# Weight loads that wait for exactly the chunk that last used their buffer; turned blocks of the up projection's first half taken one chunk on

## The chip, the cores and the metric

One core of one Trainium2 chip runs the kernel. The metric is the device time of one execution in microseconds; lower is better. The kernel before took 2496.27 us (median of three executions, 2493.42 to 2497.68).

## The reference

Two transformer blocks run one after the other on x of 256 tokens by 2048 features, all in float32. What matters here is the first block's feed-forward part, on `rms_norm(h)` of 256 x 2048:

```python
def conv_gated_mlp(u, w_up, conv_w, conv_b, w_down):
    '''up-projection -> causal depthwise conv (width 3) -> GELU gate * value -> down-projection.'''
    S = u.shape[1]
    up = u @ w_up
    pad = jnp.pad(up, ((0, 0), (CONV_WIDTH - 1, 0), (0, 0)))
    up = conv_b + sum(pad[:, j:j + S] * conv_w[j] for j in range(CONV_WIDTH))
    gate, val = jnp.split(up, 2, axis=-1)
    return (jax.nn.gelu(gate, approximate=True) * val) @ w_down
```

`w_up` is 2048 x 11264 and `w_down` is 5632 x 2048. Around it stand the mixers, output projections, an embedding gate and, in the second block, a gated feed-forward of the same size without a convolution (phase "glu" below).

## The kernel before

**Chunks.** Every weight matrix is streamed in chunks of 1 MB (128 partitions x 2048 floats; 512 input rows by 512 columns), 428 in all, grouped in phases (`PHASES`). Phase "up" has 11 iterations of 8 chunks; chunks 0 to 3 of an iteration give 512 gate columns (the first half), chunks 4 to 7 the 512 value columns (the second half). The queue SP issues the load of a chunk into one of four buffers `raw0` to `raw3` (`load`, buffer j % 4). ACT rounds it to `w_hi` (`high`, L645), DVE subtracts to get the remainder `w_lo` (`low`, L1662), and PE multiplies with both (L1208 to L1210). `w_hi` and `w_lo` have two buffers each, so ACT's copy for chunk j+2 waits until PE has finished chunk j. The stretch on ACT from that copy to the next is called slot j here; extra work given for j in a stream's `at` table runs on ACT or DVE behind slot j's copy or subtraction.

**When a load may start.** A load waits until DVE has finished the chunk `back` before it: `c - back + 1` chunks done. With four buffers the last user of a buffer is normally four chunks back. A phase whose number of chunks before it is not a multiple of four shifts this: phase "pe1" has two chunks, so the first two chunks of "up" reuse buffers whose last user is two chunks back. `stream_plan` takes for each j the smallest distance over all iterations of a phase, which for "up" gives back = [2, 2, 4, 4, 4, 4, 4, 4], in every one of its 11 iterations. Phases "pg1" and "pg2" (two iterations each) have the same list; "down1" to "down2" have 4 except where a phase begins two chunks off.

**The turned blocks.** The up projection comes out with tokens on partitions; the convolution wants columns on partitions. For each half, ACT copies the result from PSUM to `up_rows` (`up_evacuation`, L910, slots 3 and 7). DVE transposes 32 x 32 blocks (`turn_up`, L2155). SP stores the blocks to DRAM (`put_up_blocks`, L434) and reads them back rearranged with four transfers (`take_up_blocks`, L440); ACT then copies them to `ff_sum` (`up_columns`, L918). The convolution (`affine` on ACT, L929; `convolve` on DVE, L2166), the GELU (`gelu_gate`, L936), the product on POOL (`up_products`, L605), its rounding on ACT (`product_high`, L955) and its remainder on POOL (L608) follow in the next iteration.

**SP's order.** SP executes in order, and its steps for the blocks of iteration i stand among the loads of iteration i+1: load 0, put first half, load 1, take first half, loads 2 to 4, put second half, load 5, take second half, loads 6 and 7. Each load stands some four chunks ahead of its multiplication. A wait in any of these holds all that follow.

**Loops.** On SP iterations 0 and 1 of "up" are written out and the rest is a loop; on ACT iteration 0 is written out. The blocks of iteration 10 are handled among the loads of "down1", whose back is 4 everywhere.

Of the kernel before, what the change touches and what calls it, by code (L numbers as in the profile page):

```python
# [49 lines left out]
RAW = 4  # L50
# [23 lines left out]
def stream_plan():  # L74


    plan, chunk, group, used = {}, 0, 0, [0] * RAW
    last = [None] * RAW
    for name, iters, body, per in PHASES:
        uses = [len(range(s, body, RAW)) for s in range(RAW)]  # L80
        back = [RAW] * body
        for i in range(iters):
            for j in range(body):
                c = chunk + i * body + j
                if last[j % RAW] is not None:
                    back[j] = min(back[j], c - last[j % RAW])
                last[j % RAW] = c
        plan[name] = dict(iters=iters, body=body, per=per, chunk=chunk, group=group,
                          used=list(used), uses=uses, back=back)
        chunk += iters * body  # L90
        group += 2 * IN1_ROWS if name == "in1" else 6 if name == "in2" else iters * 2 if name in COLUMN_PHASES else 0
        used = [u + iters * n for u, n in zip(used, uses)]
    return plan


def two_blocks_program(nc: bass.Bass, t: dict, out: bass.AP):
    plan = stream_plan()
    ctx = ExitStack()
    with ctx:
# [5 lines left out]
        def sem(name):  # L105
            if name not in sems:
                sems[name] = ctx.enter_context(nc.semaphore(name))
            return sems[name]
# [165 lines left out]
        def chunk_no(ph, i, j):  # L274
            return plan[ph]["chunk"] + i * plan[ph]["body"] + j
# [30 lines left out]
        def _(sp):  # L306
            def weight(w, k0, nk, c0, n):
                return w.rearrange("(k p) n -> p k n", p=P)[:, k0:k0 + nk, bass.ds(c0, n)]

            def load(ph, i, j, src):  # L310
                pl = plan[ph]
                s = j % RAW
                c = chunk_no(ph, i, j)
                if not (ph == "in1" and isinstance(i, int) and i == 0 and j < RAW):
                    sp.wait_ge(sem("w_lo_ready"), c - pl["back"][j] + 1)
                k = src.shape[1]
                sp.dma_start(raw[s][:, :].rearrange("p (k n) -> p k n", k=k), src).then_inc(sem(f"raw_landed{s}"), 16)

            def columns(ph, mats, width, kts=KT, at=None, order=None, peel=0, column=None, after=None):
                def body(i):  # L320
                    for j in range(plan[ph]["body"]):
                        if at and j in at:
                            at[j](i)
                        if ph == "in1" and isinstance(i, int) and i == 0 and j < RAW:
                            continue
                        gr, q = divmod(j, kts // 4)
                        w = mats[gr]
                        if order:
                            q = order[q]
                        load(ph, i, j, weight(w[0], 4 * q, 4, (column(i) if column else i * width) + w[1], 512))  # L330
                    if after:
                        after(i)
                iterations(sp, ph, body, peel=peel, unroll=order is not None)
# [33 lines left out]
            def store_bias():  # L367

                sp.wait_ge(sem("bias_row_ready"), 1)
                sp.dma_start(bias_dram[:, 0:S + P - 1], bias_row[0:4, 0:S + P - 1]).then_inc(sem("bias_stored"), 16)  # L370

            columns("in1", [(t["w_in"][0], 0), (t["w_in"][0], 512)], 1024, peel=7,
                    column=lambda i: 1024 * IN1_ORDER[i], after=lambda i: store_bias() if i == 0 else None)
# [83 lines left out]
            def earlier(f):  # L457
# [13 lines left out]
            w = t["w_down"][0]  # L471
# [7 lines left out]
                    peel=1,  # L479
# [10 lines left out]
            for n, name in enumerate(["gmlp_ln_g_2", "gmlp_ln_b_2"]):  # L490
                sp.dma_start(ln_rows[n], t[name].broadcast_to([P, 1024])).then_inc(sem("ln_rows_landed"), 16)
            columns("in2", [(t["w_in_2"][0], 0), (t["w_in_2"][0], 512)], 1024, peel=5,
                    column=lambda i: 1024 * IN2_ORDER[i])
# [3 lines left out]
            w = t["ffn_w2_2"][0]  # L497
# [134 lines left out]
        def _(act):  # L632
# [18 lines left out]
            def token_roots(name):  # L651

                at = NORMS[name]
                act.wait_ge(sem("tokens_summed"), NORM_NO[name])
                A(tok[:, at + 10:at + 12], tok[:, at + 8:at + 10], ACT.Sqrt, bias=eps[:, 0:1], scale=1.0 / D)\
                    .then_inc(sem("tokens_rooted"), 1)
# [35 lines left out]
            def first(f):  # L692

                return lambda i: f() if isinstance(i, int) and i == 0 else None

            def stream(ph, at=None, peel=0, unroll=False, tail=0, started=False, late=False):
                at = at or {}
                last = ph == NPH[-1]
                final = (plan[ph]["iters"] - 1, plan[ph]["body"] - 1)

                def body(i):
                    for j in range(plan[ph]["body"]):
                        if not (last and i == plan[ph]["iters"] - 1 and j + SPLIT >= plan[ph]["body"]) \
                                and not (late and (i, j) == final) and not (started and isinstance(i, int) and i == 0 and j == 0):
                            high(ph, i, j + SPLIT)
                        if j in at:
                            at[j](i)
                iterations(act, ph, body, peel=peel, unroll=last or unroll, tail=tail)
# [152 lines left out]
            def done(ph, i, j):  # L861

                return chunk_no(ph, i, j) + 1
# [38 lines left out]
            def up_evacuation(i, gr):  # L902
                act.wait_ge(sem("chunks_multiplied"), done("up", i, 4 * gr + 3))
                act.wait_ge(sem("up_scale_ready"), 1)
                if isinstance(i, int) and (i, gr) == (0, 0):
                    act.wait_ge(sem("h_put0"), 16)
                else:
                    act.wait_ge(sem("blocks_turned"), i * 2 + gr)
                for a in range(2):
                    last = A(up_rows[:, a, :], bank(2 * gr + a), ACT.Copy, scale=tok[:, NORMS["up"] + 12 + a:NORMS["up"] + 13 + a])  # L910
                last.then_inc(sem("up_rows"), 1)

            def up_columns(i, gr):
                act.wait_ge(sem("blocks_loaded"), i * 128 + (64 * gr + 64))
                if not (isinstance(i, int) and i == 0):
                    act.wait_ge(*((sem("up_low"), i) if gr else (sem("up_conv0"), i * 8)))
                for a in range(2):
                    last = A(in_blocks(ff_sum[gr][:, :, a * P:(a + 1) * P]), staged_half(up_staged, a), ACT.Copy)  # L918
                last.then_inc(sem(f"up_summed{gr}"), 1)

            def affine(ph, gr):
                def f(i):

                    act.wait_ge(sem(f"{ph}_summed{gr}"), i + 1)
                    if not (isinstance(i, int) and i == 0):
                        act.wait_ge(sem("up_product"), i)
                    for n in range(4):
                        c = i * 4 + (44 * gr + n)
                        A(ff_out[gr][:, n, :], ff_sum[gr][:, n, :], ACT.Identity,  # L929
                          bias=cols[:, bass.ds(c + col["conv_b"], 1)],  # L930
                          scale=cols[:, bass.ds(c + col["conv_w2"], 1)]).then_inc(sem(f"{ph}_tap{gr}"), 1)
                return f
# [20 lines left out]
            def product_high(i):  # L953
                act.wait_ge(sem("up_product"), i + 1)
                A(g[:, bass.ds(i * 4, 4), 0:S], ff_sum[1][:, :, :], ACT.Copy).then_inc(sem("up_high"), 1)  # L955

            def earlier_high(i):
                if not (isinstance(i, int) and i == 0):
                    act.wait_ge(sem("pe_stored"), 16)
                    product_high(i - 1)  # L960

            def earlier_glu(i):
                if not (isinstance(i, int) and i == 0):
                    glu_high(i - 1)

            def earlier(f):

                return lambda i: None if isinstance(i, int) and i == 0 else f(i - 1)

            def second_values(i):  # L970
                up_columns(i, 1)
                affine("up", 1)(i)

            stream("up", {0: lambda i: (first(lambda: token_roots("up"))(i), earlier(affine("up", 0))(i)),
                          2: earlier(second_values), 3: lambda i: (up_evacuation(i, 0), earlier(gelu_gate)(i)),
                          6: lambda i: up_columns(i, 0), 7: lambda i: (up_evacuation(i, 1), earlier_high(i))},
                   peel=1, started=True)

            ups = plan["up"]["iters"]
            stream("down1", unroll=True, at={  # L980
                0: lambda i: affine("up", 0)(ups - 1),
                2: lambda i: second_values(ups - 1),
                3: lambda i: gelu_gate(ups - 1),
                6: lambda i: product_high(ups - 1),
# [1439 lines left out]
```

## Time and profile before

| | |
|---|---|
| median of three executions | 2496.27 us (2493.42 to 2497.68) |
| the profiled execution, its time | 2494.16 us |
| its span, first to last instruction | 2492.4 us |
| granted TensorE clock, mean | 0.992 |
| PE busy | 2449.3 us (98%) |
| DVE, ACT, POOL busy | 1375.7, 1182.1, 123.4 us |
| DMA | 507.20 MB, mean 203 GB/s |

The profile is of one execution. Busy time is the time in which an engine worked on instructions; matmuls overlap, and their ends are modelled. The time of the profiled execution is 1.8 us longer than its span. In the tables of waits, the engine in front of the arrow stood idle until the one behind it finished.

### The profile page before, as it was taken

Reading aid. Unit: us, or ns where it says so; the run is one execution under the profiler, and the core shown is the slowest. Engines: PE = TensorE matmul, PEld = TensorE weight load, DVE = VectorE, ACT = ScalarE, POOL = GpSimd, SP = SyncE. Lnnn points to the kernel's source line nnn. Section 1 sums busy time; section 2 is a strip of 40 time slices with the busy share of each in tenths; the row PEclk is TensorE's granted clock in tenths of the full one; section 3 lists DMA queues with packets and bytes.
Section 4 is the critical chain, followed back from the end, with each engine's and each line's share of the span. In section 5 each row is a group of like instructions: output and inputs, shape, how many; then the busy total and the mean of one; then the engine's idle time right before and its main releaser. Section 6 shows DMA issues by size and latency. Waiting matters only on the chain.

```text
span 2492.4 us, 29186 instructions
## 1 busy us (share of the span) xinstructions
PE 2449.3 (98%) x11800; PEld 2061.8 (83%) x11800; DVE 1375.7 (55%) x1109; ACT 1182.1 (47%) x1092; POOL 123.4 (5%) x140
## 2 busy tenths in 40 slices
PE   9999999999999999999999999999999999999998
PEld 8999888877777777888888889888888888888886
DVE  6877644655555556544556575654454545444445
ACT  5533654655555665433454354544334343433344
POOL 4000000001001101100000000000000010000000
PEclk9999999999999999999999999999999999999999
DMA  7545455567757758855466554556666666665544
GB/s 257 187 157 168 162 181 186 211 209 238 227 174 241 242 185 263 290 193 195 165 241 227 179 177 153 185 186 206 215 220 216 221 214 215 213 234 186 190 179 154
DMA packets 256579, 507.20 MB, mean 203 GB/s; under 512 B 10422, under 2 KB 30828, under 8 KB 255596
## 3 DMA queue, kind: packets, MB, share of 16 engines
q1 hardware_dynamic: 256056, 505.64, 60.5%
q8 instruction: 66, 1.08, 0.2%
q10 hardware_dynamic: 436, 0.30, 0.0%
q14 instruction: 21, 0.17, 0.0%
HBM read 480.73 MB, written 25.17 MB: 203 GB/s over the span
## 4 chain that ended last, share of the span: by engine, by line
PE 86%; DMA 5%; ACT 4%; DVE 2%; issue 1%; SPq 1%; ACTq 0%; DVEq 0%
PE ps L1208 24%; PE ps L1210 23%; PE ps L1209 23%; PE ps L1193 4%; DMA up_turned_rows<-h 3%; DMA h<-up_turned_rows 3%; DVE w_lo L1662 2%; PE ps L1194 2%; ACT w_hi L645 2%; PE ps L1201 2%; PE ps L1202 2%; PE ps L1200 2%; PE ps L1166 1%; PE ps L1453 1%; SPq L440 1%
## 5 line engine op out<-in xcount | busy, mean ns | idle before, releaser
L1662 DVE TENSOR_TENSOR w_lo<-raw,w_hi 128x2048 fp32r<-128x2048 f32 x427 | 988.2, 2314 | 1072.4 <-ACT w_hi L645 1071.9
L645 ACT ACTIVATE w_hi<-raw 128x2048 fp32r<-128x2048 f32 x427 | 818.2, 1916 | 1200.5 <-PE ps L1210 1018.5
L1208 PE MATMUL ps<-w_hi,xa 128*128 128x512 f32 x1728 | 681.3, 394 | 28.5 <-DVE w_lo L1662 28.5
L1210 PE MATMUL ps<-w_hi,xa 128*128 128x512 f32 x1728 | 678.3, 393 | 0.0
L1209 PE MATMUL ps<-w_lo,xa 128*128 128x512 f32 x1728 | 677.7, 392 | 0.0
L1208 PE MATMUL ps<-w_hi,g 128*128 128x512 f32 x1216 | 475.2, 391 | 0.0
L1210 PE MATMUL ps<-w_hi,g 128*128 128x512 f32 x1216 | 473.3, 389 | 0.0
L1209 PE MATMUL ps<-w_lo,g 128*128 128x512 f32 x1216 | 473.1, 389 | 0.0
L1208 PEld LDWEIGHTS ps<-w_hi,xa 128*128 128x128 f32 x1728 | 328.4, 190 | 101.9 <-DVE w_lo L1662 32.7
L1210 PEld LDWEIGHTS ps<-w_hi,xa 128*128 128x128 f32 x1728 | 327.4, 189 | 69.2
L1209 PEld LDWEIGHTS ps<-w_lo,xa 128*128 128x128 f32 x1728 | 328.3, 190 | 67.7
L1208 PEld LDWEIGHTS ps<-w_hi,g 128*128 128x128 f32 x1216 | 228.3, 188 | 48.0 <-issue 1.3
L1210 PEld LDWEIGHTS ps<-w_hi,g 128*128 128x128 f32 x1216 | 228.3, 188 | 47.4
L1209 PEld LDWEIGHTS ps<-w_lo,g 128*128 128x128 f32 x1216 | 228.4, 188 | 46.6
L1193 PE MATMUL ps<-xa,w_hi 128*128 128x512 f32 x256 | 89.8, 396 | 0.1
L1193 PE MATMUL ps<-g,w_hi 128*128 128x512 f32 x256 | 89.9, 395 | 0.0
L614 POOL TENSOR_TENSOR g<-ff,g 128x512 f32 x22 | 36.7, 1690 | 753.9 <-ACT g L950 753.9
L2166 DVE SCALAR_TENSOR_TENSOR ff<-ff,cols 128x255 f32<-128x255 f32 (+1 forms) x176 | 73.0, 477 | 0.0
L1200 PE MATMUL ps<-xa,w_hi 128*128 128x256 f32 x256 | 72.8, 285 | 0.0
L1202 PE MATMUL ps<-xa,w_lo 128*128 128x256 f32 x256 | 72.5, 283 | 0.0
L1201 PE MATMUL ps<-xa,w_hi 128*128 128x256 f32 x256 | 72.4, 283 | 0.0
L1194 PE MATMUL ps<-g,w_lo 128*128 128x256 f32 x256 | 71.6, 280 | 0.0
(321 smaller groups left out, 1674.2 us busy)
## 6 DMA issues: line engine op xcount, KB each, us to landing
raw<-in_ffn_w_dram SPq DMA_DIRECT2D x132, 1024.0 KB, 5.1
raw<-in_w_in_dram SPq DMA_DIRECT2D x95, 1024.0 KB, 5.0
raw<-in_w_up_dram SPq DMA_DIRECT2D x88, 1024.0 KB, 6.8
raw<-in_w_down_dram SPq DMA_DIRECT2D x44, 1024.0 KB, 5.1
raw<-in_w_out_dram SPq DMA_DIRECT2D x32, 1024.0 KB, 5.1
raw<-in_w_pg_dram SPq DMA_DIRECT2D x16, 1024.0 KB, 6.7
raw<-in_pl_w_gate_dram SPq DMA_DIRECT2D x16, 1024.0 KB, 6.3
up_turned_rows<-h SPq DMA_DIRECT2D x22, 512.0 KB, 3.2
```

The source lines that it names most:

```text
L614: last = pool.tensor_tensor(in_blocks(g[:, bass.ds(i * 4, 4), S + a * P:S + (a + 1) * P]), staged_half(staged, a), in_blocks(g[:, bass.ds( ...
L645: A(w_hi[j % SPLIT][:, :], raw[s][:, :], ACT.Copy).then_inc(sem("w_hi_ready"), 1)
L1193: mm(ps[:, 4 * gr + n, :], hi[:, k, w], x, start=begin, stop=False)
L1194: return mm(ps[:, 4 * gr + n, 0:S], lo[:, k, w], x[:, 0:S], start=False, stop=end)
L1200: mm(o, hi[:, k, w], x[:, 0:S], start=begin and n % 2 == 0, stop=False, skip_group_check=True)
L1201: mm(o, hi[:, k, w], x[:, S:2 * S], start=False, stop=False, skip_group_check=True)
L1202: return mm(o, lo[:, k, w], x[:, 0:S], start=False, stop=end, skip_group_check=True)
L1208: mm(o, high, hi, start=begin, stop=False)
L1209: mm(o, high, lo, start=False, stop=False)
L1210: return mm(o, low, hi, start=False, stop=end)
L1662: V.tensor_tensor(w_lo[j % SPLIT][:, :], raw[j % RAW][:, :], w_hi[j % SPLIT][:, :].bitcast(F32), ALU.subtract).then_inc(sem("w_lo_ready"), 1)
L2166: V.scalar_tensor_tensor(ff_out[gr][:, n, tap:S], ff_sum[gr][:, n, 0:S - tap], cols[:, bass.ds(c, 1)], ff_out[gr][:, n, tap:S], ALU.mult, ...
```

## The change

Two edits. First, `back` becomes two lists for each phase, one for iteration 0 and one for all later ones, so that for "up", "pg1" and "pg2" chunks 0 and 1 of every iteration after the first wait for the chunk four back. A loop that isn't peeled still takes the smaller of the two. Twenty loads in "up" and two each in "pg1" and "pg2" have a different threshold; no load is added or moved in SP's order.

Second, on ACT: `up_columns` of the first half goes from slot 6 to slot 7, ahead of `up_evacuation` of the second half; `product_high` goes from slot 7 to slot 0 of the next iteration, behind `affine`; and two iterations are written out instead of one.

```diff
--- before.py
+++ after.py
@@ -78,12 +78,12 @@
     last = [None] * RAW
     for name, iters, body, per in PHASES:
         uses = [len(range(s, body, RAW)) for s in range(RAW)]
-        back = [RAW] * body
+        back = [[RAW] * body for _ in range(2)]
         for i in range(iters):
             for j in range(body):
                 c = chunk + i * body + j
                 if last[j % RAW] is not None:
-                    back[j] = min(back[j], c - last[j % RAW])
+                    back[min(i, 1)][j] = min(back[min(i, 1)][j], c - last[j % RAW])
                 last[j % RAW] = c
         plan[name] = dict(iters=iters, body=body, per=per, chunk=chunk, group=group,
                           used=list(used), uses=uses, back=back)
@@ -307,12 +307,14 @@
             def weight(w, k0, nk, c0, n):
                 return w.rearrange("(k p) n -> p k n", p=P)[:, k0:k0 + nk, bass.ds(c0, n)]
 
-            def load(ph, i, j, src):
+            def load(ph, i, j, src, peeled=True):
                 pl = plan[ph]
                 s = j % RAW
                 c = chunk_no(ph, i, j)
                 if not (ph == "in1" and isinstance(i, int) and i == 0 and j < RAW):
-                    sp.wait_ge(sem("w_lo_ready"), c - pl["back"][j] + 1)
+                    back = pl["back"][i > 0][j] if isinstance(i, int) else \
+                        pl["back"][1][j] if peeled else min(pl["back"][0][j], pl["back"][1][j])
+                    sp.wait_ge(sem("w_lo_ready"), c - back + 1)
                 k = src.shape[1]
                 sp.dma_start(raw[s][:, :].rearrange("p (k n) -> p k n", k=k), src).then_inc(sem(f"raw_landed{s}"), 16)
 
@@ -327,7 +329,7 @@
                         w = mats[gr]
                         if order:
                             q = order[q]
-                        load(ph, i, j, weight(w[0], 4 * q, 4, (column(i) if column else i * width) + w[1], 512))
+                        load(ph, i, j, weight(w[0], 4 * q, 4, (column(i) if column else i * width) + w[1], 512), peel > 0)
                     if after:
                         after(i)
                 iterations(sp, ph, body, peel=peel, unroll=order is not None)
@@ -954,31 +956,30 @@
                 act.wait_ge(sem("up_product"), i + 1)
                 A(g[:, bass.ds(i * 4, 4), 0:S], ff_sum[1][:, :, :], ACT.Copy).then_inc(sem("up_high"), 1)
 
-            def earlier_high(i):
-                if not (isinstance(i, int) and i == 0):
-                    act.wait_ge(sem("pe_stored"), 16)
-                    product_high(i - 1)
-
             def earlier_glu(i):
                 if not (isinstance(i, int) and i == 0):
                     glu_high(i - 1)
 
-            def earlier(f):
-
-                return lambda i: None if isinstance(i, int) and i == 0 else f(i - 1)
+            def earlier(f, n=1):
+
+                return lambda i: None if isinstance(i, int) and i < n else f(i - n)
 
             def second_values(i):
                 up_columns(i, 1)
                 affine("up", 1)(i)
 
-            stream("up", {0: lambda i: (first(lambda: token_roots("up"))(i), earlier(affine("up", 0))(i)),
+            def product_high_stored(i):
+                act.wait_ge(sem("pe_stored"), 16)
+                product_high(i)
+
+            stream("up", {0: lambda i: (first(lambda: token_roots("up"))(i), earlier(affine("up", 0))(i), earlier(product_high_stored, 2)(i)),
                           2: earlier(second_values), 3: lambda i: (up_evacuation(i, 0), earlier(gelu_gate)(i)),
-                          6: lambda i: up_columns(i, 0), 7: lambda i: (up_evacuation(i, 1), earlier_high(i))},
-                   peel=1, started=True)
+                          7: lambda i: (up_columns(i, 0), up_evacuation(i, 1))},
+                   peel=2, started=True)
 
             ups = plan["up"]["iters"]
             stream("down1", unroll=True, at={
-                0: lambda i: affine("up", 0)(ups - 1),
+                0: lambda i: (affine("up", 0)(ups - 1), product_high(ups - 2)),
                 2: lambda i: second_values(ups - 1),
                 3: lambda i: gelu_gate(ups - 1),
                 6: lambda i: product_high(ups - 1),
```

The rows below are ACT's instructions in the loop of "up", from slot 6 on, in the kernel before. `w_hi0<-raw0` is slot 6's copy, `ff<-h` is `up_columns`, `h<-ps,tok` is `up_evacuation`, `g<-ff` is `product_high`.

```order
L645 ACTIVATE w_hi0<-raw0 128x2048 [waits chunks_multiplied]
L914 ISA
L918 ACTIVATE ff<-h 128x4x128 [waits up_conv0,blocks_loaded]
L918 ACTIVATE ff<-h 128x4x128
L644 REGISTER_ALU [waits raw_landed1]
L645 ACTIVATE w_hi1<-raw1 128x2048 [waits chunks_multiplied]
L903 REGISTER_ALU
L908 REGISTER_ALU [waits up_scale_ready,chunks_multiplied]
L910 ACTIVATE h<-ps,tok 128x512 [waits blocks_turned]
L910 ACTIVATE h<-ps,tok 128x512
L955 ISA [waits up_product,pe_stored]
L955 ACTIVATE g<-ff 128x4x256
```

The same place in the changed kernel:

```order
L647 ACTIVATE w_hi0<-raw0 128x2048 [waits chunks_multiplied]
L646 REGISTER_ALU [waits raw_landed1]
L647 ACTIVATE w_hi1<-raw1 128x2048 [waits chunks_multiplied]
L916 ISA
L920 ACTIVATE ff<-h 128x4x128 [waits up_conv0,blocks_loaded]
L920 ACTIVATE ff<-h 128x4x128
L905 REGISTER_ALU
L910 REGISTER_ALU [waits up_scale_ready,chunks_multiplied]
L912 ACTIVATE h<-ps,tok 128x512 [waits blocks_turned]
L912 ACTIVATE h<-ps,tok 128x512
```

`up_columns` now stands behind the second of the two weight copies instead of between them, still ahead of the evacuation; `product_high` has gone from here.

The head of the same loop on ACT, slot 0, before (`ff<-ff,cols` is `affine`, of which the first of four is shown):

```order
L644 ISA [waits raw_landed2]
L645 ACT_TABLE_LOAD
L645 ACTIVATE w_hi0<-raw2 128x2048 [waits chunks_multiplied]
L926 REGISTER_ALU [waits up_summed0]
L929 ISA [waits up_product]
L929 REGISTER_ALU
L929 ACTIVATE ff<-ff,cols 128x256
```

The same head in the changed kernel, to the next weight copy:

```order
L646 ISA [waits raw_landed2]
L647 ACTIVATE w_hi0<-raw2 128x2048 [waits chunks_multiplied]
L928 REGISTER_ALU [waits up_summed0]
L931 ISA [waits up_product]
L931 REGISTER_ALU
L931 ACTIVATE ff<-ff,cols 128x256
```

and, further down to the next copy,

```order
L931 ACTIVATE ff<-ff,cols 128x256
L957 ISA [waits up_product,pe_stored]
L957 ACTIVATE g<-ff 128x4x256
L646 REGISTER_ALU [waits raw_landed3]
L647 ACTIVATE w_hi1<-raw3 128x2048 [waits chunks_multiplied]
```

`product_high` stands at the end of slot 0, and the load of an activation table ahead of slot 0's weight copy is gone. The loop's other table load, ahead of the GELU in slot 3, is gone as well. Slot 3 before:

```order
L645 ACTIVATE w_hi1<-raw1 128x2048 [waits chunks_multiplied]
L910 ACTIVATE h<-ps,tok 128x512 [waits blocks_turned,up_scale_ready,chunks_multiplied]
L910 ACTIVATE h<-ps,tok 128x512
L935 ISA
L936 ACT_TABLE_LOAD
L936 ACTIVATE ff<-ff 128x1024 [waits up_conv0]
```

and in the changed kernel:

```order
L647 ACTIVATE w_hi1<-raw1 128x2048 [waits chunks_multiplied]
L912 ACTIVATE h<-ps,tok 128x512 [waits blocks_turned,up_scale_ready,chunks_multiplied]
L912 ACTIVATE h<-ps,tok 128x512
L937 ISA
L938 ACTIVATE ff<-ff 128x1024 [waits up_conv0]
```

What moved here is only that table load: it now stands once, in the written-out iteration 1.

## Rows read from the trace of the kernel before

**Rows 1.** Page, part 1: busy time, share of the span and instructions of each engine

```profile
PE 2449.3 (98%) x11800; PEld 2061.8 (83%) x11800; DVE 1375.7 (55%) x1109; ACT 1182.1 (47%) x1092; POOL 123.4 (5%) x140
```

**Rows 2.** Waits, whole span: who waited for whom; us in total, times, longest

```profile
ACT ff L918 <- DMA h<-up_turned_rows: 63.7, 10, 7.9
...
PE ps L1208 <- DVE w_lo L1662: 28.5, 12, 4.3
```

**Rows 3.** Timeline of PE: start us, us, what, [idle before <-releaser]; first and last restart

```profile
522.85 0.50 PE L1208 MATMUL ps<-w_hi,xa 128*128 128x512 f32 x1 [4.32 <-DVE w_lo L1662]
...
955.54 0.50 PE L1208 MATMUL ps<-w_hi,xa 128*128 128x512 f32 x1 [1.58 <-DVE w_lo L1662]
```

**Rows 4.** Windows: stretch, its length, busy us of each engine, PEclk, DMA, GB/s

```profile
571.00:619.00 48.00, 45.31 (x192) 37.02 (x192) 27.79 (x29) 28.29 (x29) 4.79 (x2) 0.96 0.68 219
1700.00:1743.50 43.50, 43.50 (x194) 36.03 (x193) 20.96 (x12) 17.52 (x12) 3.40 (x2) 1.00 0.68 218
```

**Rows 5.** Timeline of ACT in the glu loop, one iteration apart

```profile
1738.22 1.92 ACT L645 ACTIVATE w_hi<-raw 128x2048 fp32r<-128x2048 f32 x1 [2.48 <-PE ps L1210]
...
1781.74 1.92 ACT L645 ACTIVATE w_hi<-raw 128x2048 fp32r<-128x2048 f32 x1 [2.48 <-PE ps L1210]
```

**Rows 6.** Timeline of ACT, up loop: slots 6, 7 and 0

```profile
847.75 1.92 ACT L645 ACTIVATE w_hi<-raw 128x2048 fp32r<-128x2048 f32 x1 [3.52 <-PE ps L1210]
855.34 1.15 ACT L918 ACTIVATE ff<-h 128x512 f32<-128x512 f32 x2 [5.67 <-DMA h<-up_turned_rows]
856.40 1.90 ACT L645 ACTIVATE w_hi<-raw 128x2048 fp32r<-128x2048 f32 x1
858.20 1.24 ACT L910 ACTIVATE h<-ps,tok 128x512 f32<-128x512 f32 x2
859.34 1.05 ACT L955 ACTIVATE g<-ff 128x1024 f32 x1
860.41 1.28 ACT L645 ACT_TABLE_LOAD   x1
...
863.52 2.07 ACT L929 ACTIVATE ff<-ff,cols 128x256 f32<-128x256 f32 x4
```

**Rows 7.** Timeline of DVE in the same iteration

```profile
835.59 1.30 DVE L2155 STREAM_TRANSPOSE h<-h 128x512 f32<-128x512 f32 x2
838.82 2.29 DVE L1662 TENSOR_TENSOR w_lo<-raw,w_hi 128x2048 fp32r<-128x2048 f32 x1 [1.93 <-ACT w_hi L645]
...
858.33 2.29 DVE L1662 TENSOR_TENSOR w_lo<-raw,w_hi 128x2048 fp32r<-128x2048 f32 x1 [5.57 <-ACT w_hi L645]
```

**Rows 8.** Timeline of the SP queue in the same iteration

```profile
841.28 0.37 SPq L317 DMA_DIRECT2D raw<-in_w_up_dram  x1
841.81 0.40 SPq L434 DMA_DIRECT2D up_turned_rows<-h  x1
...
848.22 1.76 SPq L440 DMA_DIRECT2D h<-up_turned_rows  x4
```

**Rows 9.** Timeline of the SP queue, last iteration of up

```profile
977.69 0.35 SPq L434 DMA_DIRECT2D up_turned_rows<-h  x1
...
980.67 1.75 SPq L440 DMA_DIRECT2D h<-up_turned_rows  x4
```

**Rows 10.** Timeline of ACT, last iteration of up: blocks of the first half

```profile
990.35 1.13 ACT L918 ACTIVATE ff<-h 128x512 f32<-128x512 f32 x2
```

**Rows 11.** Timeline of POOL and DVE where both run

```profile
988.99 2.42 POOL L605 TENSOR_TENSOR ff<-ff 128x1024 f32<-128x1024 f32 x1 [31.06 <-DVE ff L2166]
...
990.48 3.07 DVE L1662 TENSOR_TENSOR w_lo<-raw,w_hi 128x2048 fp32r<-128x2048 f32 x1 [1.57 <-ACT w_hi L645]
...
1034.11 2.29 DVE L1662 TENSOR_TENSOR w_lo<-raw,w_hi 128x2048 fp32r<-128x2048 f32 x1 [2.38 <-ACT w_hi L645]
...
1035.30 3.36 POOL L608 TENSOR_TENSOR g<-ff,g 128x1024 f32 x1 [5.72 <-ACT g L955]
```

**Rows 12.** Transfers that write or read up_turned_rows: from issue to landing

```profile
DMA to landing us min/median/max: 3.0/4.4/7.9
```

## The prediction

> **What bounds the kernel now.** The page gives PE 98% of the span [rows 1], so only PE's pauses and what they do to its clock can be won. The waits name one pause that counts: PE stood for 28.5 us in 12 waits for `w_lo`, and ACT for 63.7 us in 10 waits for the turned blocks [rows 2]. Ten of the twelve PE waits are in "up", one for each of iterations 0 to 9; the first and the last are in [rows 3]: 4.32 us and 1.58 us. The lines in between repeat the pattern.
>
> The timelines of one iteration show the mechanism. ACT's copy of slot 6 starts at 847.75 and ends at 849.67. Then ACT stands 5.67 us for the first half's blocks and takes them at 855.34. Slot 7's copy, due 5.44 us after slot 6's, at 853.19, starts at 856.40, 3.21 us late [rows 6]. Its `w_lo` starts at 858.33 [rows 7], and PE, which asks for that chunk one chunk later, has stopped. The spare room is about 1 us: from the start of a copy (856.40) to the end of its `w_lo` (858.33 + 2.29) are 4.22 us, of a slot of 5.44, of which PE's own lead takes some 0.2.
>
> Why are the blocks late? DVE has them transposed at 835.59 + 1.30 = 836.89 [rows 7]. SP issues their store only at 841.81, since load 0 stands ahead of it and goes at 841.28 [rows 8]. That is right behind the `w_lo` of the chunk two back (838.82 + 2.29 = 841.11 [rows 7]): the threshold of back = 2. The store, behind 1 MB of weights issued 0.5 us earlier, takes 848.22 - 841.81 = 6.41 us until the read goes.
>
> The pause also costs clock. The window of a whole iteration has PEclk 0.96, one of glu, where nothing pauses, has 1.00 [rows 4]. So the stretches after pauses ran partly at 1.2 instead of 2.4 GHz, and the loss per iteration is more than the recorded idle.
>
> **The change part by part.** *What an undisturbed iteration takes.* Glu streams the same 8 chunks an iteration (192 and 194 matmuls stand in the windows [rows 4]), and its loop repeats every 1781.74 - 1738.22 = 43.52 us [rows 5], 5.44 a chunk. In "up" the restarts of PE go from 522.85 to 955.54 [rows 3], nine iterations in 432.69 us, 48.08 each. The difference is 4.56 us in each of nine. Rough check by windows: 48 us with 45.31 of busy PE leaves 2.7 idle, and 45.31 - 43.50 = 1.8 is the slower clock [rows 4]; together 4.5.
>
> *The loads' threshold.* With back = 4, load 0 waits for a `w_lo` two chunks earlier, two slots of 5.44 before 841.11, so it is out of the way and the store goes at about 836.9, 4.9 us earlier. The last iteration of "up" already runs so, because its blocks are handled among the loads of "down1": store at 977.69, read at 980.67, 2.98 us later instead of 6.41 [rows 9], and ACT takes the blocks at 990.35 with no wait on its line [rows 10]. For the traced iteration the read would be issued at 836.9 + 2.98 = 839.9, or with the old 6.41 at 843.3, and with its old 7.1 us to the use (855.34 - 848.22) the blocks are there at 847.0 to 850.4. In slot 6 ACT would ask at 849.67: at worst 0.7 us late, inside the room of 1 us.
>
> *The move of `up_columns`.* In slot 7 ACT asks at 853.19 + 1.92 = 855.1. The blocks then have 4.7 to 8.1 us to spare; even at the old 855.34 they would be only 0.2 us late. Either edit alone takes away nearly the whole pause, so their effects don't add. Slot 7 holds 1.92 + 1.15 + 1.24 = 4.31 us of 5.44 [rows 6]. The second half's evacuation, 1.15 us later than it would be undisturbed, delays its transposes, their store and read by as much. That is the price I had to check: transposes end near slot 0's start + 0.3, the read's last part is issued near + 0.3 + 2.98 + 1.75 = 5.0 [rows 9], and transfers land in 3.0 to 7.9, median 4.4 [rows 12], so at 8.0 to 12.9. ACT asks in slot 2 at 2 x 5.44 + 1.92 = 12.8. The longest landing just touches it.
>
> *The move of `product_high`* (1.05 us [rows 6]): slot 0 then holds 1.92 + 2.07 + 1.05 = 5.04 of 5.44 us. Its source, POOL's product, ended at 988.99 + 2.42 = 991.41 [rows 11], more than two chunks before it is read. Its successor, POOL's L608, must be done before slot 2's `up_columns` writes `ff_sum`: 5.04 + 0.3 + 2.4 = 7.7 against 12.8. Cost nothing, hidden beside PE's chunk; without this cover it would cost 1.05 us per iteration.
>
> *The table loads*: two of 1.28 us [rows 6] leave nine iterations. Both lie in ACT's idle time once nothing is late; I take zero. They give slot 3 back 1.3 us of room.
>
> *Loads 2 to 7* stand behind the blocks' steps; with these earlier, none is later against its chunk. In "pg1" and "pg2" four loads may go earlier, but of the 12 waits [rows 2] none lies there; zero.
>
> *Sum.* First pause 4.32, nine iterations 9 x 4.56 = 41.0, together 45.3 us. The profiled execution took 2494.16, its span 2492.4. 2494.16 - 45.3 = 2448.9. The median shown is 2.1 above the profiled one: 2496.27 - 45.3 = 2451.0, which I predict.
>
> **A rule against it.** POOL's L608 now starts at slot 0 + 5.3 and ends at + 7.7, and slot 1's `w_lo` is due at 5.44 + 1.95 = 7.4; before, it met a transposition. Where POOL ran first, `w_lo` took 3.07 instead of 2.29 and ended at 993.55, 2.14 after POOL's end at 991.41; where DVE ran first, POOL took 3.36 instead of 2.42 [rows 11]. So the later one seems to be held until the earlier one ends. That would hold slot 1's `w_lo` by 0.3 us, inside the room.
>
> The Trainium skill, "SBUF — State Buffer", section "Who interferes with whom", says that a DVE instruction with two SBUF inputs and a reading GpSimd instruction exclude each other for the whole instruction. By that rule, the trace agrees.
>
> **The rivals.** *(a) Forecast*, no pause left in iterations 0 to 9: 2451. Chance 0.82.
>
> *(b) POOL meets `w_lo`.* If slot 0 runs late by up to 2 us, L608 starts just ahead of slot 1's `w_lo` and holds it for nearly 2.4 us, 1.4 beyond the room, in nine iterations, with about 1.8 of slow clock each: 29 us given back, 2480. Against it: 5.04 us fit a slot, as slot 2's do now. It decides from 0.8 us of lateness on. Chance 0.05.
>
> *(c) The second half's blocks are late in slot 2*, or iteration 0's behind the 2 MB store of the embedding. Each late us beyond 1.2 costs 1 plus the clock; 1 us too late in nine iterations is 9 x 2.8 = 25, 2476; in only a few of them 2 to 10, 2453 to 2461. For it: the longest landing of 7.9; against it: the median of 4.4. Chance 0.09.
>
> *(d) The earlier loads change nothing* and the blocks stay as late, with a wait of the same length in slot 7: within 5 us of 2496. The last iteration [rows 9, 10] speaks against it. Chance 0.02.
>
> *(e) Slower.* In slot 7 the evacuation is queued behind the wait for the blocks. The same bytes in less time are more traffic (219 GB/s x 48/43.5 = 242, an estimate from [rows 4]). A lateness L against the asking at 855.1 costs L less the slot's free 5.44 - 4.31 = 1.1 and the room of 1, and 1.8 of clock. It passes the present 4.56 from L = 4.9 on, blocks 4.6 us later than now. At L = 7 it is 2.1 us more in each of nine iterations: 2496 + 19 = 2515. The last iteration's 2.98 us from store to read is strongly against it. Chance 0.02.
>
> **How the numbers follow.** Three executions before spread by 4.3 us, so 0.2% (5 us) is about what can be told from no change. Faster by more than that: (a), (b), (c), 0.96; same 0.02; slower 0.02. The range starts at 2446, the sum with the faster executions, and reaches to 2463, the end of the few-iterations case of (c) with its noise: it leaves out (b), the heavy case of (c), (d) and (e), about 0.15.
>
> **What would show it.** PE's waits in "up" gone, PEclk 1.00 there, its iterations 43.5 us. SP issues the first half's store right behind DVE's transposes, with the read some 3 us later. ACT takes these blocks in slot 7 without a wait, and no wait appears in slot 2. No table load in the loop. I am wrong if PE waits for `w_lo` in chunks 2 or 3 of the iterations (then (c) or (b)), or if the store still goes behind load 0.

## The result and the profile after

The changed kernel takes 2449.28 us (median of four, 2448.87 to 2449.34); the kernel before, run beside it, 2494.85 us (2488.75 to 2497.68). The ratio is 0.982, 95% interval 0.9801 to 0.9839. The profiled execution took 2449.34 us, 44.8 us less than the profiled one of before; the working expected 45.3 less. Forecast was 2451.

The page of the kernel after, part 1:

```profile
PE 2430.4 (99%) x11800; PEld 2050.7 (84%) x11800; DVE 1376.4 (56%) x1109; ACT 1156.9 (47%) x1073; POOL 124.0 (5%) x140
```

PE is busy 18.9 us less than in [rows 1]. It had no work taken from it (11800 matmuls in both): the matmuls that followed a pause at the lower clock are short now. The rest of the 44.8 us, 25.9, is idle time of PE that is gone.

The waits of the kernel after, whole span. The line for `w_lo` stood at 28.5 us in [rows 2]; a line for ACT's wait for the turned blocks does not occur:

```profile
PE ps L1209 <- DVE w_lo L1663: 0.8, 2, 0.5
```

The windows of the kernel after: the same first stretch of the loop cut to one undisturbed iteration, and all of iterations 2 to 9 (columns as in [rows 4]):

```profile
571.00:614.50 43.50, 43.50 (x193) 35.98 (x193) 27.89 (x29) 25.68 (x26) 4.83 (x2) 1.00 0.75 242
571.00:956.00 385.00, 385.00 (x1699) 318.55 (x1699) 248.30 (x251) 225.59 (x228) 40.95 (x17) 1.00 0.75 240
```

PE is busy in every microsecond of these 385, at full clock. From one copy of slot 7 to that of the next iteration (818.64 to 862.16) are 43.52 us.

ACT's timeline in one iteration of the kernel after, from slot 6's copy to slot 1's; this is the place of [rows 6]:

```profile
813.20 1.92 ACT L647 ACTIVATE w_hi<-raw 128x2048 fp32r<-128x2048 f32 x1 [3.52 <-PE ps L1211]
818.64 1.92 ACT L647 ACTIVATE w_hi<-raw 128x2048 fp32r<-128x2048 f32 x1 [3.52 <-PE ps L1211]
820.46 1.13 ACT L920 ACTIVATE ff<-h 128x512 f32<-128x512 f32 x2
821.50 1.25 ACT L912 ACTIVATE h<-ps,tok 128x512 f32<-128x512 f32 x2
824.08 1.92 ACT L647 ACTIVATE w_hi<-raw 128x2048 fp32r<-128x2048 f32 x1 [1.33 <-PE ps L1211]
825.90 2.06 ACT L931 ACTIVATE ff<-ff,cols 128x256 f32<-128x256 f32 x4
827.86 1.05 ACT L957 ACTIVATE g<-ff 128x1024 f32 x1
829.52 1.92 ACT L647 ACTIVATE w_hi<-raw 128x2048 fp32r<-128x2048 f32 x1 [0.60 <-PE ps L1211]
```

The copies stand 5.44 us apart and each waits for PE, never for a transfer. The blocks (L920, 820.46) are taken the moment slot 7's copy is through. Slot 0 has `product_high` (L957) at its end, and 0.60 us are left to it.

The SP queue of the kernel after, and DVE's transposes of the first half, to be set beside [rows 7, 8]:

```profile
802.36 0.35 SPq L436 DMA_DIRECT2D up_turned_rows<-h  x1
802.97 0.37 SPq L319 DMA_DIRECT2D raw<-in_w_up_dram  x1
805.48 1.76 SPq L442 DMA_DIRECT2D h<-up_turned_rows  x4
```

```profile
801.03 1.30 DVE L2156 STREAM_TRANSPOSE h<-h 128x512 f32<-128x512 f32 x2
...
831.47 2.29 DVE L1663 TENSOR_TENSOR w_lo<-raw,w_hi 128x2048 fp32r<-128x2048 f32 x1 [3.15 <-ACT w_hi L647]
```

The transposes end at 801.03 + 1.30 = 802.33 and the store is issued at 802.36, 0.03 us later; before, it was 4.92 us later. From the store's issue to the read's (805.48) are 3.12 us instead of 6.41. No weight load is issued just ahead of the store any more; load 1 follows it. Run e9 below, where load 0 stands ahead of it again, has the long time again.

### The profile page after: what moved, and what is told of

It is laid out like the page before. It is cut to its first block, busy times and chain, and to the rows that moved or that the text cites. A ratio compares the mean times of both kernels' runs of the same rounds, so it can differ in the third digit from the quotient of the medians.

```text
span 2447.6 us, 29160 instructions
## 1 busy us (share of the span) xinstructions
PE 2430.4 (99%) x11800; PEld 2050.7 (84%) x11800; DVE 1376.4 (56%) x1109; ACT 1156.9 (47%) x1073; POOL 124.0 (5%) x140
## 4 chain that ended last, share of the span: by engine, by line
PE 98%; ACT 1%; DVE 0%; DMA 0%; issue 0%; SPq 0%; DVEq 0%; ACTq 0%
PE ps L1209 27%; PE ps L1211 27%; PE ps L1210 27%; PE ps L1194 4%; PE ps L1195 2%; PE ps L1202 2%; PE ps L1203 2%; PE ps L1201 2%; PE ps L1167 1%; PE ps L1454 1%; ACT w_hi L647 0%; DMA raw<-in_w_in_dram 0%; DVE w_lo L1663 0%; PE ps L1461 0%; PE ps L1602 0%
## 5 line engine op out<-in xcount | busy, mean ns | idle before, releaser
L647 ACT ACTIVATE w_hi<-raw 128x2048 fp32r<-128x2048 f32 x427 | 818.5, 1917 | 1244.4 <-PE ps L1211 1059.0
L1209 PE MATMUL ps<-w_hi,xa 128*128 128x512 f32 x1728 | 673.7, 390 | 0.8 <-DVE w_lo L1663 0.8
L1211 PE MATMUL ps<-w_hi,xa 128*128 128x512 f32 x1728 | 672.4, 389 | 0.0
L1209 PEld LDWEIGHTS ps<-w_hi,xa 128*128 128x128 f32 x1728 | 324.3, 188 | 69.0 <-DVE w_lo L1663 0.9
L1211 PEld LDWEIGHTS ps<-w_hi,xa 128*128 128x128 f32 x1728 | 324.3, 188 | 67.7
```

The costliest lines, as they stand in the source:

```text
L647: A(w_hi[j % SPLIT][:, :], raw[s][:, :], ACT.Copy).then_inc(sem("w_hi_ready"), 1)
L1209: mm(o, high, hi, start=begin, stop=False)
L1211: return mm(o, low, hi, start=False, stop=end)
```

## The experiments

Times are medians; the kernel before ran on the same chip beside each group.

| kernel | us | its before | ratio, 95% interval |
|---|---|---|---|
| e1 loads only | 2449.79 | 2491.68 | 0.9831 (0.9814 to 0.9847) |
| e2 ACT only | 2452.00 | 2491.68 | 0.9835 (0.9818 to 0.9852) |
| e3 two written out | 2491.70 | 2491.68 | 1.0006 (0.9992 to 1.0020) |
| e4 blocks moved only | 2460.72 | 2491.68 | 0.9874 (0.9857 to 0.9890) |
| e6 moved, no table loads | 2453.85 | 2489.02 | 0.9855 (0.9830 to 0.9879) |
| e5 store held, behind load 1 | 2449.02 | 2496.66 | 0.9803 (0.9777 to 0.9829) |
| e7 store held, behind load 2 | 2487.96 | 2496.66 | 0.9959 (0.9948 to 0.9970) |
| e8 load 0 exact | 2461.19 | 2496.66 | 0.9853 (0.9826 to 0.9879) |
| e9 load 1 exact | 2459.71 | 2496.66 | 0.9843 (0.9816 to 0.9867) |
| e10 changed again | 2449.48 | 2489.02 | 0.9838 (0.9813 to 0.9862) |

The executions of the kernel before spread by 9 to 12 us within a group, and those of e3 by 12; those of all the others by 0.5 to 5. So these others are compared with each other by their own times. The changed kernel came out within 0.2 us of itself in two groups (2449.28 and 2449.48).

**The first edit alone (e1).** ACT's order is that of before. The two lists of `back` are as in the change; of the edit only the line that waits is shown:

```diff
-                    sp.wait_ge(sem("w_lo_ready"), c - pl["back"][j] + 1)
+                    back = pl["back"][i > 0][j] if isinstance(i, int) else \
+                        pl["back"][1][j] if peeled else min(pl["back"][0][j], pl["back"][1][j])
+                    sp.wait_ge(sem("w_lo_ready"), c - back + 1)
```

> Only the loads' threshold is changed; ACT's order is that of before. My theory (all of the gain is the pause behind ACT's wait for the first half's blocks in slot 6): the store goes some 5 us earlier, the blocks are there when slot 6 asks, no pause is left in iterations 0 to 9, 2449 us, at most 2 us more. Rival A (the place where ACT asks is what counts): a pause stays in most iterations, 2460 to 2475 us. Rival B (the two table loads in the loop count): some 2470 us.

2449.79 us, and between 571 and 956 us PE is busy without a gap. ACT's timeline, slots 6 and 7:

```profile
813.67 1.92 ACT L647 ACTIVATE w_hi<-raw 128x2048 fp32r<-128x2048 f32 x1 [3.52 <-PE ps L1212]
815.49 1.13 ACT L920 ACTIVATE ff<-h 128x512 f32<-128x512 f32 x2
819.11 1.92 ACT L647 ACTIVATE w_hi<-raw 128x2048 fp32r<-128x2048 f32 x1 [2.49 <-PE ps L1212]
...
823.15 1.28 ACT L647 ACT_TABLE_LOAD   x1
824.61 1.92 ACT L647 ACTIVATE w_hi<-raw 128x2048 fp32r<-128x2048 f32 x1 [0.17 <-PE ps L1212]
```

The blocks are taken in slot 6, right behind its copy, with no idle time ahead of them. The table load (L647, 823.15) is still there and fits. The theory held; both rivals fell. The first edit alone gives all of the gain that can be told from noise: its four executions took 2449.33 to 2451.32 us, those of the changed kernel 2448.87 to 2449.72.

**The second edit alone (e2).** The changed kernel with `back` computed as before, one list for all iterations.

> Only ACT's part is changed (blocks of the first half in slot 7, product in slot 0, two iterations written out); the loads wait as before. My theory: the store goes as late as before, the read lands 0.2 to 2.4 us after slot 7 asks, of which a slot with 1.1 us free and 1 us of room swallows all but a few tenths in a few iterations: 2449 to 2455 us. The chain of waits for the blocks stays visible on ACT, some 0.2 to 2 us in ten places, but not on PE. Rival A (the blocks' lateness decides wherever they are asked for): over 2475 us.

2452.00 us, inside the range. But the wait that is left is not the one I expected. The waits of this kernel between 516 and 1000 us:

```profile
ACT w_hi L645 <- DMA raw<-in_w_up_dram: 45.1, 13, 6.3
...
PE ps L1207 <- DVE w_lo L1661: 3.1, 3, 1.7
...
ACT ff L918 <- DMA h<-up_turned_rows: 1.5, 4, 0.6
```

For the turned blocks ACT waits 1.5 us in 4 places. For weights it waits in 13, ten of them at slot 7's copy, which needs chunk 1's weights; load 1 is issued late under back = 2. One iteration of ACT:

```profile
858.95 1.92 ACT L645 ACTIVATE w_hi<-raw 128x2048 fp32r<-128x2048 f32 x1 [3.52 <-PE ps L1209]
865.32 1.92 ACT L645 ACTIVATE w_hi<-raw 128x2048 fp32r<-128x2048 f32 x1 [4.45 <-DMA raw<-in_w_up_dram]
867.14 1.13 ACT L918 ACTIVATE ff<-h 128x512 f32<-128x512 f32 x2
...
869.83 1.92 ACT L645 ACTIVATE w_hi<-raw 128x2048 fp32r<-128x2048 f32 x1 [0.41 <-PE ps L1209]
```

The copy starts at 865.32, 6.37 us after slot 6's instead of 5.44, so 0.9 us late; in the other iterations of the loop it is 0.1 to 2.0 us late. In the kernel before, this lateness lay under the longer one of the blocks. PE lost 3.1 us in three places, one of 1.73 us (in iteration 0), where I had expected a few tenths.

**Table loads alone (e3).** On ACT `peel=1` becomes `peel=2`, nothing else.

> The kernel before with two iterations of the loop written out on ACT instead of one, which takes both table loads out of the loop and does nothing else. My theory: 2495 us, as before, within 0.2%. Rival (the table loads lie on the path): two of 1.28 us in nine iterations, 23 us less, 2472 us.

2491.70 us, ratio 1.0006: the two table loads lay in idle time. The theory held.

**The blocks' place alone (e4).** The rest is as before.

```diff
-                          6: lambda i: up_columns(i, 0), 7: lambda i: (up_evacuation(i, 1), earlier_high(i))},
+                          7: lambda i: (up_columns(i, 0), up_evacuation(i, 1), earlier_high(i))},
```

> The kernel before with the first half's blocks taken in slot 7 and nothing else: the product's rounding stays in slot 7 and a table load ahead of slot 0's copy. My theory: slot 7 then holds 1.92 + 1.15 + 1.24 + 1.05 = 5.36 us, with the table load 6.64 of 5.44, and the blocks come 0.2 to 2.4 us late; so slot 0's copy is 1.4 to 3.6 us late against 1 us of room, and PE pauses 0.4 to 2.6 us in ten iterations, with slow clock behind some: 2460 to 2485 us. Rival (moving the question alone is enough): 2449 to 2453 us.

2460.72 us, at the low end of what was expected, and well over the rival's. The pauses are fewer and shorter than expected: in the profiled execution (2456.65 us, the fastest of the four) PE waits 3.8 us in 8 places, at most 0.9, with no slow clock behind them. The cause is partly another one: ACT waits 0.8 us in 4 places for the blocks and 33.6 us in 8 for chunk 1's weights. Then slot 7 is too full:

```profile
824.64 1.92 ACT L645 ACTIVATE w_hi<-raw 128x2048 fp32r<-128x2048 f32 x1 [4.84 <-DMA raw<-in_w_up_dram]
826.46 1.13 ACT L918 ACTIVATE ff<-h 128x512 f32<-128x512 f32 x2
827.50 1.25 ACT L910 ACTIVATE h<-ps,tok 128x512 f32<-128x512 f32 x2
828.64 1.05 ACT L955 ACTIVATE g<-ff 128x1024 f32 x1
829.71 1.28 ACT L645 ACT_TABLE_LOAD   x1
831.00 1.92 ACT L645 ACTIVATE w_hi<-raw 128x2048 fp32r<-128x2048 f32 x1
```

Slot 7's copy is 1.3 us late (824.64, 6.76 after slot 6's at 817.88) and its work, with `product_high` (L955) and the table load, runs to 831.00. Slot 0's copy, due two slots after slot 6's at 828.76, is 2.2 us late.

**The same without the table loads (e6).** `peel=2` is added to the last.

> The kernel of the fourth run (first half's blocks taken in slot 7, loads as before, product's rounding still in slot 7) with two iterations written out, so without the table loads in the loop. If the 1.28 us table load ahead of slot 0's copy is what overfilled slot 7 there, slot 7 now holds 5.36 of 5.44 us, only the late weight load of chunk 1 (0.1 to 1.3 us after slot 7's copy is due) is left, and the room of 1 us takes it: 2451 to 2455 us, against 2460.7. Rival (the product's rounding must leave slot 7): 2458 to 2461 us.

2453.85 us, as expected. So of the 8.7 us between the kernel with the blocks' place alone and the whole second edit (2452.00), removing the table loads gives 6.9. The other 1.9 would be `product_high`'s, but e6 and e2 stand in different groups and e2's own executions run from 2449.48 to 2453.05, so these 1.9 are not shown.

**Store held back, twice (e5, e7).** Both start from the changed kernel. The first:

```diff
-                    at={1: earlier(lambda i: put_up_blocks(i - 1, 0)), 2: earlier(lambda i: take_up_blocks(i - 1, 0)),
+                    at={2: earlier(lambda i: (sp.wait_ge(sem("w_lo_ready"), chunk_no("up", i - 1, 7) + 1),
+                                             put_up_blocks(i - 1, 0), take_up_blocks(i - 1, 0))),
```

> The changed kernel, with the first half's store and read put behind load 1 and held until the remainder of the chunk three ahead of load 2's (chunk 7 of the iteration whose blocks they are) is made: the store goes at about the w_lo end of slot 5, 46.6 on the clock of the traced iteration of before against its 41.8, read issued 3 to 6.4 us later, blocks there 4 to 6 us after that, so 0 to 5 us after slot 7 asks. Price by my rule: a lateness L costs L less 2.1, and 1.8 of slow clock where the pause is long. Expected L about 1.5 to 2.5, so pauses of 0 to 0.5 us: 2449 to 2456 us. Rival (lateness passes straight on, as it did in slot 6 less 1 us): L less 1 in ten iterations plus clock, 2465 us or more.

2449.02 us and no wait for the blocks at all. SP's queue and ACT:

```profile
855.82 0.35 SPq L436 DMA_DIRECT2D up_turned_rows<-h  x1
858.46 1.76 SPq L442 DMA_DIRECT2D h<-up_turned_rows  x4
```

```profile
862.35 1.92 ACT L648 ACTIVATE w_hi<-raw 128x2048 fp32r<-128x2048 f32 x1 [3.52 <-PE ps L1212]
864.17 1.13 ACT L921 ACTIVATE ff<-h 128x512 f32<-128x512 f32 x2
```

The store takes 2.64 us, where I had expected 3 to 6.4. The read takes at most 864.17 - 858.46 = 5.71 from its issue, inside the 4 to 6 that I had expected; in the traced iteration of before it took 7.1. So it was the store's time that I had too long. With no weight load just ahead of the store and the read, even a store that goes 4.9 us later against slot 6's copy than in the kernel before is in time for slot 7.

The second puts them at `3:` and holds them to `chunk_no("up", i, 0) + 1`.

> The same, held one chunk longer (until chunk 0's remainder of the next iteration is made) and put behind load 2, so that no weight load is held up ahead of it. Store 10 us later than in the kernel before, as in my slower rival. Blocks 5.9 to 7.5 us after slot 7 asks. By my rule a pause of 3.8 to 5.4 and 1.8 of clock in ten iterations, 5.6 to 7.2 each: 2505 to 2521 us, slower than the kernel before. Rival (a later place of asking absorbs most of it): under 2480 us.

2487.96 us: much slower than the changed kernel, but still 0.4% faster than the kernel before, not slower as I expected. ACT and PE:

```profile
842.65 1.92 ACT L648 ACTIVATE w_hi<-raw 128x2048 fp32r<-128x2048 f32 x1 [3.52 <-PE ps L1212]
849.27 1.15 ACT L921 ACTIVATE ff<-h 128x512 f32<-128x512 f32 x2 [4.70 <-DMA h<-up_turned_rows]
...
851.47 1.91 ACT L648 ACTIVATE w_hi<-raw 128x2048 fp32r<-128x2048 f32 x1
```

```profile
855.76 0.51 PE L1210 MATMUL ps<-w_hi,xa 128*128 128x512 f32 x1 [2.27 <-DVE w_lo L1664]
...
856.92 0.63 PE L1210 MATMUL ps<-w_hi,xa 128*128 128x512 f32 x1
```

The blocks are 4.70 us late, not 5.9 to 7.5: the store took 2.65 us (issued at 842.35) and the read 4.3 (issued at 845.00). My rule, lateness less 2.1, gives 2.6; PE paused 2.27. This iteration is 903.40 - 855.76 = 47.64 us, 4.12 above 43.52, so 1.9 us are clock (the matmul at 856.92 shows 0.63 us, usual is 0.39). The rule for the price held within 0.3 us; the input to it, the durations of the transfers, was off. With the lateness that it had, the rule gives 2.6 + 1.8 = 4.4 us for an iteration, just under the 4.56 of the kernel before, and e7 came out 8.7 us below that kernel.

**One load at a time (e8, e9).** ACT as before. In the first, load 0 alone gets the exact threshold; in the second, load 1 alone. What the first adds to e1's edit:

```diff
+                    if j == 1:
+                        back = min(pl["back"][0][j], pl["back"][1][j])
                     sp.wait_ge(sem("w_lo_ready"), c - back + 1)
```

(the second has `j == 0` there.)

> ACT as before (blocks asked for in slot 6). Only load 0 of each iteration waits for the chunk four back; load 1 still for the chunk two back. My theory: the store goes early, but the read stands behind load 1 in SP's order and goes only 1 us earlier than before; the blocks come with it, about 3 to 4 us after slot 6 asks, less crowded by the store: pauses of 1 to 3 us: 2470 to 2490 us. Rival (only the store's time counts): 2449 us.

> ACT as before. Only load 1 waits for the chunk four back; load 0 still for the chunk two back. The store goes as late as before, behind load 0; load 1 goes 4 us earlier, right behind the store, and is done sooner than the read needs the engines. My theory: the read is issued at the same time as before and lands at most 1 to 2 us earlier: 2475 to 2492 us. Rival (the weights of chunk 1 are what slot 7 waits for): 2449 us.

2461.19 and 2459.71 us. Both missed: neither the expected times nor the rivals'. In both the mechanism is the expected one, and the price is smaller. ACT in the first, SP in the second:

```profile
820.82 1.92 ACT L649 ACTIVATE w_hi<-raw 128x2048 fp32r<-128x2048 f32 x1 [3.52 <-PE ps L1214]
827.20 1.15 ACT L922 ACTIVATE ff<-h 128x512 f32<-128x512 f32 x2 [4.46 <-DMA h<-up_turned_rows]
828.26 1.90 ACT L649 ACTIVATE w_hi<-raw 128x2048 fp32r<-128x2048 f32 x1
```

```profile
814.38 0.37 SPq L321 DMA_DIRECT2D raw<-in_w_up_dram  x1
814.91 0.40 SPq L438 DMA_DIRECT2D up_turned_rows<-h  x1
815.56 0.37 SPq L321 DMA_DIRECT2D raw<-in_w_up_dram  x1
821.46 1.76 SPq L444 DMA_DIRECT2D h<-up_turned_rows  x4
```

With load 0 exact, the store goes early, but the read stands behind load 1 and is issued only 1.0 us earlier against slot 6's copy than before. Slot 7's copy is 2.00 us late (828.26 against 820.82 + 5.44) and PE paused 0.88 us. With load 1 exact the store still takes 6.55 us behind load 0, but the blocks were taken at 826.79, 5.33 us after the read's issue instead of 7.12, since load 1 is out of its way; slot 7's copy is 1.56 us late and PE pauses 0.4 us (in other iterations up to 1.96). The traced iteration of before has 3.21 us late and 2.08 us of pause. All three say that 1.1 us are swallowed. So the two loads share the fault: load 0 holds up the store, load 1 the read, and each alone put right gives 35 to 37 of the 47 us; the gains don't add. What fell is the price: the iterations with load 0 exact are 44.75 us on average (nine from PE's restart at 519.41 to that at 922.18), 1.23 above 43.52, for pauses of 0.90. The windows of e8, then of the kernel before, show why:

```profile
571.00:956.00 385.00, 377.75 (x1657) 309.95 (x1656) 241.75 (x247) 242.62 (x240) 38.82 (x17) 1.00 0.71 236
```

```profile
571.00:956.00 385.00, 364.31 (x1538) 297.57 (x1539) 223.58 (x226) 227.52 (x226) 38.84 (x17) 0.96 0.68 218
```

With pauses of 0.9 us the clock stayed at its upper level, PEclk 1.00, and PE had 7 us idle. With those of the kernel before it was 0.96, and the same 385 us hold 1538 matmuls instead of 1657.

**The changed kernel again (e10)**, beside e6.

> The changed kernel once more, as a yardstick on the same chip: 2449 us, no PE wait for a remainder in the loop of the up projection.

2449.48 us, with no such wait of PE between 516 and 1000 us.

## Why the prediction was right

*What bounds the kernel*: right. Ten pauses behind ACT's wait for the turned blocks; with that wait gone (e1) all ten are gone, with it moved (e2) seven are and three short ones are left. The iteration went from 48.08 to 43.52 us, which was [rows 5]'s figure carried over from another phase.

*The sum*: 45.3 us expected, 44.8 found between the two profiled executions. These 0.5 us mean nothing: PE's restart after its short wait in iteration 0 stands at 485.64 in the trace of before, at 486.42 in that of after and anywhere from 485.29 (e9) to 486.73 (e10) in the others, so executions differ by more than that ahead of the first pause. One term didn't come: the 2.1 us by which the median of before lay above its profiled execution were carried over into the forecast of 2451.0. The changed kernel has hardly any such spread (0.5 us in four executions), and the sum without them, 2448.9, is the nearer one.

*The threshold*: store expected at the transposes' end, found 0.03 us behind it; store to read 2.98 expected from the last iteration, 3.12 found. The last iteration of "up" was a sample of the changed thresholds inside the trace of before, and the best evidence. What the step called "at worst" wasn't: it took the 7.1 us from the read to the use from one iteration, and in the kernel before they run from 6.7 to 8.8. And it spoke of load 0 only; e9 shows that load 1, issued 1.5 us ahead of the read, had a part as large.

*The move of `up_columns`, and "either edit alone takes away nearly the whole pause, so their effects don't add"*: right, 2449.8 and 2452.0. What this step missed is the second lateness: under back = 2 load 1 brings its weights after slot 7's copy is due, 0.9 us in the iteration shown of e2, 1.3 in that of e4. I wrote of the loads only as what stands ahead of the blocks. It is why the second edit alone is 2.5 us short of the whole, and part of why the blocks' move without the table loads' removal and `product_high`'s move is 11 us short (e4).

*The move of `product_high` and the table loads at zero*: right for the changed kernel and for the kernel before (e3). The room that they leave around slot 7 is worth about 7 us (the table loads) to 9 (both) if the blocks' place moves and the loads stay as they were (e4, e6, e2); with the exact threshold, and the blocks in slot 6, the kernel does without it (e1).

*The rule against it*: POOL's L608 (L610 in the changed kernel) was forecast at slot 0 + 5.3 to + 7.7 and ran from 829.19 to 831.59, + 5.1 to + 7.5. It met slot 1's `w_lo` for 0.1 us only; that `w_lo` starts at 831.47, 7.39 after slot 0's copy, and takes its usual 2.29 us.

*Rivals*: (b), (c), (d) and (e) did not come. The slower one is what e7 goes towards: its pause is real and follows the rule. It was to pass the kernel before from a lateness of 4.9 us on; e7 had 4.7 and stayed just below it, with a store 11 us later than before against slot 6's copy. Slower than the kernel before was not reached in any run. The price that (c) named, 1 us and 1.8 of clock for each late us, was too high for short pauses: those of 0.9 us in e8 cost 1.2 each.

## What to carry to other kernels

A threshold that is right for the first iteration and applied to all of them shows up not at the load that it delays but at whatever is queued behind it: here a 512 KB store stood 4.9 us behind a load whose buffer had long been free, and the read took 7.1 us instead of 5.3 with the second such load just ahead of it (e9). Compare a loop's period with the same work where nothing waits (another phase, the last iteration) before summing idle times; the sum of recorded pauses (28.5 us) was over a third short of the 44.8 us gained, since PE was also busy for 18.9 us less once the slower clock behind them was gone. And when one wait hides another, test each edit alone before calling one of them idle: the one that was hidden decides how much slack the other edit needs.

## What the runs showed of the hardware

The cost of a pause of PE is not in proportion. Pauses of 0.8 to 1.0 us in ten iterations cost 1.2 us each with PEclk 1.00 (e8). Pauses of 2.2 us in e7 cost 4.1 us where the lower clock followed, as in the kernel before, and 2.6 where it did not. PE's restarts in three iterations of e7 that follow each other:

```profile
666.74 0.50 PE L1210 MATMUL ps<-w_hi,xa 128*128 128x512 f32 x1 [2.22 <-DVE w_lo L1664]
...
712.82 0.79 PE L1210 MATMUL ps<-w_hi,xa 128*128 128x512 f32 x1 [2.21 <-DVE w_lo L1664]
...
760.45 0.74 PE L1210 MATMUL ps<-w_hi,xa 128*128 128x512 f32 x1 [2.19 <-DVE w_lo L1664]
```

The first iteration, 46.08 us, is 2.56 above 43.52 and ran at PEclk 1.00; the second, 47.63 us, is 4.11 above it and ran at 0.96. With pauses of one length the lower clock alone cost 1.55 us.

Nor does the length alone decide whether the clock falls. In e9 the matmuls behind a pause of 1.96 us ran at the lower clock (0.63 us each). In the kernel with two iterations written out (e3), matmuls behind a pause of 2.65 us ran at the full clock, and those behind one of 2.41 us did not. PE's timeline of e3, first the restart behind 2.65 us (PEclk 1.00 from 709.4 to 715), then that behind 2.41 us with a matmul of 0.63 us at the lower clock (PEclk 0.70 from 949.4 to 955):

```profile
709.42 0.50 PE L1208 MATMUL ps<-w_hi,xa 128*128 128x512 f32 x1 [2.65 <-DVE w_lo L1662]
```

```profile
949.46 0.50 PE L1208 MATMUL ps<-w_hi,xa 128*128 128x512 f32 x1 [2.41 <-DVE w_lo L1662]
...
950.28 0.63 PE L1208 MATMUL ps<-w_hi,xa 128*128 128x512 f32 x1
```

This fits the spread of the times. The kernel before, with pauses of 1.6 to 4.3 us, spreads by 9 to 12 us from run to run; e7, with pauses of 2.2 us in all but the first iteration, by 2.5; the changed kernel by 0.5. That the spread comes from the pauses and from what the clock adds to them is argued, not shown: only one execution of each kernel has a trace.

A store of 512 KB took 6.3 to 6.6 us to the read's issue when a 1 MB load was issued 0.5 us ahead of it (before, e9). It took 3.0 to 3.1 in the changed kernel, where the last load was issued about 6 us ahead and the next 0.6 us behind, and 2.6 to 2.7 in the first halves of e5 and e7, with the last load over 10 us ahead and none behind until the read was out. Behind three loads issued together it is in between: the second halves' stores of e5, 5.8 us after the last of them, took 4.2 to 4.5 in the loop. The read of the same blocks took 6.7 to 8.8 us with a load 1.5 us ahead (before), 5.3 in all but one iteration of e9, whose last load was issued 5.9 us ahead, and 4.2 to 4.3 in the loop of e7, where only later loads were near. That differs by more than I allowed for when I took the durations of before for the experiments.
